# One pass over both expert tables for two of five blocks, in place of their row gathers

## The reference, cut to what matters

```python
q = (xs @ w_pq).reshape(PEER_BLOCK, PEER_HEADS, 2, PEER_QDIM // 2)
sc = jnp.einsum('thpd,hpnd->thpn', q, sub_keys)
s, i = lax.top_k(sc, PEER_TOPK)
cidx = i[:, :, 0, :, None] * PEER_KEYS + i[:, :, 1, None, :]
top, sel = lax.top_k(cand, PEER_TOPK)
eidx = jnp.take_along_axis(cidx, sel, axis=-1)
g = jax.nn.softmax(top, axis=-1)
hid = jnp.einsum('td,thkd->thk', xs, u_tab[eidx])
a = g * jax.nn.gelu(hid)
return jnp.einsum('thk,thkd->td', a, v_tab[eidx])
```

## Time and profile before

| what | value |
|---|---|
| median of 3 runs | 1980.1 us (1979.33 to 1987.95) |
| profiled execution, first to last instruction (span) | 1895.5 us |
| profiled execution, own time | not given apart; the span and what lies around it are compared with the median |
| PE busy, share of the span | 1601.3 us, 84% |
| DVE busy | 1263.2 us, 67% |
| ACT busy | 627.4 us, 33% |
| POOL busy | 1245.3 us, 66% |
| data moved | 744.60 MB, mean 393 GB/s |
| granted TensorE clock, mean | 0.964 |

### The profile page before, as it was taken

One profiled execution on the slowest core, in us unless ns is written; L12 is line 12 of the kernel. 1 busy time (PEld: TensorE's weight loads), 2 busy tenths in 40 slices (PEclk: granted clock), 3 DMA queues, 4 the chain that ended last, 5 costly groups with the idle time before them and its releaser, 6 DMA issues.

```text
span 1895.5 us, 20537 instructions
## 1 busy us (share of the span) xinstructions
PE 1601.3 (84%) x6192; PEld 881.4 (47%) x6192; DVE 1263.2 (67%) x2836; ACT 627.4 (33%) x1771; POOL 1245.3 (66%) x1199
## 2 busy tenths in 40 slices
PE   8999779879978698888898889998689877767877
PEld 7596445536435355355354465634436422222322
DVE  2379984576767755868587647589756897655543
ACT  1432561223237422232276222136522232222211
POOL 3027676576677755777777665677777777777771
PEclk9999999999989999999999998998899999999999
DMA  9899999999999999999999999999999999999995
GB/s 318 309 347 371 410 393 387 410 409 409 386 412 409 409 401 409 406 408 409 411 406 393 397 406 377 406 409 370 405 411 409 409 410 409 409 409 409 410 409 225
DMA packets 210197, 744.60 MB, mean 393 GB/s; under 512 B 24640, under 2 KB 29544, under 8 KB 209960
## 3 DMA queue, kind: packets, MB, share of 16 engines
q0 software_dynamic: 166720, 605.75, 80.9%
q1 hardware_dynamic: 43368, 137.53, 19.0%
HBM read 736.03 MB, written 7.75 MB: 392 GB/s over the span
## 4 chain that ended last, share of the span: by engine, by line
DMA 35%; PE 30%; POOL 20%; issue 9%; DVE 6%; ACT 1%; SPq 0%; DVEq 0%; ACTq 0%
DMA vbuf<-in_peer_v,idx 18%; PE acc L959 10%; POOL ubuf L1670 9%; POOL vbuf L1670 8%; DMA ubuf<-in_peer_u,idx 8%; PE mixer L667 5%; DMA held<-in_peer_u,idx 4%; PE mixer L833 2%; PE mixer L936 2%; DVE ubuf L1598 2%; PE mixer L683 2%; DMA wring<-in_c_k 1%; POOL wring L1670 1%; DMA held<-in_peer_v,idx 1%; POOL held L1670 1%
## 5 line engine op out<-in xcount | busy, mean ns | idle before, releaser
L959 PE MATMUL acc<-vbuf,diag 128*128 128x512 f32 x1308 | 644.5, 627 | 159.5 <-DMA vbuf<-in_peer_v,idx 154.6
L1670 POOL DMA_INDIRECT ubuf<-in_peer_u,idx x518 | 553.9, 1069 | 255.5 <-issue 138.4
L1670 POOL DMA_INDIRECT vbuf<-in_peer_v,idx x478 | 512.4, 1072 | 264.4 <-PE acc L959 133.0
L1598 DVE CUSTOM_DVE_ANT_0 ubuf<-ubuf,x 128x1024 f32<-128x1024 f32 x332 | 404.9, 1224 | 252.9 <-DMA ubuf<-in_peer_u,idx 249.7
L959 PEld LDWEIGHTS acc<-vbuf,diag 128*128 128x128 f32 x1308 | 236.7, 196 | 470.4 <-issue 429.0
L1598 DVE CUSTOM_DVE_ANT_0 ubuf<-ubuf,mixer 128x1024 f32<-128x1024 f32 x186 | 225.6, 1218 | 118.2 <-DMA ubuf<-in_peer_u,idx 81.9
L1200 ACT ACTIVATE act_h<-hid 128x4 f32<-128x4 f32 x144 | 29.5, 205 | 504.1 <-DVE hid L1598 503.4
L936 PEld LDWEIGHTS mixer<-stage,wring 128*128 128x128 f32 x1280 | 149.5, 193 | 17.4 <-issue 15.4
L936 PE MATMUL mixer<-stage,wring 128*128 128x128 f32 x1280 | 150.6, 276 | 0.7 <-DMA wring<-in_w_pq 0.6
L1229 ACT ACTIVATE diag<-ident,coef 128x128 f32<-128x128 f32 x392 | 138.4, 395 | 22.1 <-PE acc L959 18.1
L1610 DVE SCALAR_TENSOR_TENSOR y_acc<-vbuf,coef,y_acc 128x1024 f32<-128x1024 f32 x99 | 127.3, 1286 | 18.1 <-DMA vbuf<-in_peer_v,idx 16.0
(11 more groups left out here) (266 smaller groups left out, 1959.1 us busy)
## 6 DMA issues: line engine op xcount, KB each, us to landing
wring<-in_w_pq SPq DMA_DIRECT2D x80, 512.0 KB, 8.1
wring<-in_w_qk SPq DMA_DIRECT2D x66, 512.0 KB, 7.6
wring<-in_w_out SPq DMA_DIRECT2D x40, 512.0 KB, 7.5
wring<-in_w_v SPq DMA_DIRECT2D x20, 512.0 KB, 7.5
ubuf<-in_peer_u,idx POOLq DMA_INDIRECT x518, 13.0
vbuf<-in_peer_v,idx POOLq DMA_INDIRECT x478, 12.7
wring<-in_c_k SPq DMA_DIRECT2D x8, 512.0 KB, 6.9
wring<-in_c_v SPq DMA_DIRECT2D x8, 512.0 KB, 7.9
```

Of the source, the lines that this page charges most:

```text
L959: last = pe.matmul(sums[hf], diags[D_PLAN[n][0]], v_buf[b][:, hf * 512:(hf + 1) * 512], start=first, stop=last_one)
L1598: nc.vector.tensor_tensor_reduce(out=u, in0=u, in1=x, scale=1.0, scalar=0.0, op0=ALU.mult, op1=ALU.add, accum_out=hid[:, k % MARKS:k % MAR ...
L1670: pool.indirect_dma_start(buf, None, a[table], bass.IndirectOffsetOnAxis(ap=idx[p % 2][:, at:at + 1], axis=0)).then_inc(landed_, 16)
```

## The change

Blocks 2 and 3 are no longer gathered. Slots remain for blocks 0, 1 and SMP (`GATHERED`), so `JSLOTS` is 2 x 128 + 64 = 320. For blocks 2 and 3 (`DENSE`, 256 frames together) a new lane "d" reads both tables once, as 128 tiles of 128 experts each. All mixers move forward: each takes 51 slots, SMP 60, and the pass begins at mark `SWEEP = 219` and ends at mark 323. Before it, in marks 198 to 219, the first part of the gates is built.

The gates of the pass are a matrix over 256 frames and 16384 experts, held in `big` for 52 tiles at a time and filled in four chunks of tiles (0 to 43, 44 to 71, 72 to 99, 100 to 127). For each chunk there are 64 groups of 4 frames. DVE makes one-hot rows `hot_j` (128 x 512) and `hot_i` (128 x 4w, w being the width of the chunk) by comparing with `iota`; one of two groups is scaled by the gate on DVE, the other on ACT; PE multiplies them (4 products with w columns), and ACT copies the result into `big`. `hot_j` has two buffers and `hot_i` three. Chunks 1 to 3 run inside the pass, in 22 tiles each.

`held` shrinks to one tile (`HELD = 1`). The room comes from `kv`, `q_pad` and `sub_k`, which are now parts of `big`. The sample's search takes 4 rounds in place of 8, with its halves of heads on halves of the partitions. v rows of slots from 206 on all go to DVE. The constant rows of the second LayerNorm are made once.

The core of the diff (lane names and marks, the sweep on each engine):

```diff
-HELD = 4
+HELD = 1
+GATHERED = (0, 1, SMP)
+DENSE = (2, 3)
+LAST_Q = len(GATHERED) - 1
+JSLOTS = LAST_Q * SLOTS + DEC
+SWEEP = 219
+MERGE = (SLOTS, SWEEP - V_LAG - 2)
 def on_tensor(k):
+    q = part_of(k)
+    return q < LAST_Q and q * SLOTS + 3 <= k < MERGE[q]
-BLOCK_1 = (5, 26), (26, 54), (54, 65), (65, 81), (70, 122)
-BLOCKS = (-30, 6), (6, 46), (46, 60), (60, 78), (66, 121)
+STAGES = {
+    1: ((5, 17), (17, 35), (35, 45), (45, 56), (48, 90)),
+    2: ((56, 68), (68, 86), (86, 96), (96, 107), (99, 141)),
+    3: ((107, 119), (119, 137), (137, 147), (147, 158), (150, 192)),
+    SMP: ((158, 170), (170, 197), (197, 207), (207, 218), (216, 242)),
+}
+CHUNKS = ((0, 44), (44, 72), (72, 100), (100, P))
+TOK = 4
+DRING_T = 7
+M_LAG, V_LAG_D = 2, 4
+def sweep_users():
+    users = [("t", q, 0) for q in range(len(DENSE))] + [("", 0, 0)] * 4 + [("g", 0, k) for k in range(GROUPS_D)]
+    users += [("x", 0, hf) for hf in range(2)]
+    for n in range(P + V_LAG_D):
+        if n + 1 < P:
+            users += [("x", n + 1, hf) for hf in range(2)]
+        users.append(("h", n, 0))
+        for c, (lo, hi) in enumerate(CHUNKS[1:], 1):
+            first, last = hi - HOMES + M_LAG, lo - 1
+            if first <= n <= last:
+                a, b = ((n + d - first) * GROUPS_D // (last + 1 - first) for d in (0, 1))
+                users += [("g", c, k) for k in range(a, b)]
...
+            def gains(u):
+                g_, w = G_INDEX[u], CHUNKS[u[1]][1] - CHUNKS[u[1]][0]
+                pe.wait_ge(hot_done, g_ + 1)
+                if g_ % 2 == 0:
+                    pe.wait_ge(hot_scaled, g_ // 2 + 1)
+                bank = bank_free(u)
+                for t in range(TOK):
+                    last = pe.matmul(bank[:, t * w:(t + 1) * w], hot_j[g_ % 2][:, t * P:(t + 1) * P],
+                                     hot_i[g_ % 3][:, t * w:(t + 1) * w], start=True, stop=True)
+            def turn_u(u):
+                raw = landed_tile("u", u[1])
+                bank = bank_free(u)
+                for c in range(4):
+                    at = (4 * u[2] + c) * P
+                    last = pe.transpose(bank[:, c * P:(c + 1) * P], raw[:, at:at + P], ident[:, :])
+            def hidden(u):
+                w = uT[u[1] % 2]
+                pe.wait_ge(bank_out, BANK_AT["x", u[1], 1] + 1)
+                bank = bank_free(u)
+                for c in range(KT):
+                    last = pe.matmul(bank[:, 0:DBLK], w[:, c * P:(c + 1) * P], x1T[:, c, :], start=c == 0, stop=c == KT - 1)
+            def spread(n):
+                w = landed_tile("v", n)
+                pe.wait_ge(mult_done, n + 1)
+                for q in range(len(DENSE)):
+                    for hf in range(2):
+                        last = pe.matmul(acc_d[q][hf], acts[n % ARING][:, q * P:(q + 1) * P], w[:, hf * 512:(hf + 1) * 512],
+                                         start=False, stop=n == P - 1)
...
+            def hots(u):
+                if g_ >= 2:
+                    dve.wait_ge(bank_done, BANK_AT[G_USERS[g_ - 2]] + 1)
+                nc.vector.tensor_tensor(hot_j[g_ % 2].rearrange("p (t n) -> p t n", n=P),
+                                        jig[:, 1, t0:t0 + TOK].unsqueeze(2).broadcast_to([P, TOK, P]),
+                                        iota[:, :].unsqueeze(1).broadcast_to([P, TOK, P]), ALU.is_equal)
...
+                        elif u[0] == "x":
+                            last = nc.scalar.copy(uT[u[1] % 2][:, u[2] * 512:(u[2] + 1) * 512], bank)
...
+                        else:
+                            last = nc.scalar.activation(acts[u[1] % ARING], bank[:, 0:DBLK], ACT.Gelu)
```

More of the change, by code:

```diff
@@ L139, with ring_plan @@
     PE_COUNT.append(PE_COUNT[-1] + on_tensor(_k))
-def ring_plan(count, first, more):
-    order, had, last, plan, n = list(range(first)), {}, {}, [], first
-    more = dict(more)
+def ring_plan(count, size, fewer_from):
+    order, had, last, plan = list(range(size)), [0] * size, [None] * size, []
     for k in range(count):
-        if k in more:
-            order = list(range(n, n + more[k])) + order
-            n += more[k]
+        if k == fewer_from:
+            order.remove(size - 1)
         b = order.pop(0)
         order.append(b)
[L152 to L160, removed]
+        plan.append((b, last[b], had[b]))
+        last[b], had[b] = k, had[b] + 1
+    return plan, last[size - 1]
+U_PLAN, U_LAST = ring_plan(JSLOTS, URING, SWEEP - 4)
+V_PLAN, V_LAST = ring_plan(JSLOTS, VRING, SWEEP - 4 - V_AT)
+D_PLAN, _ = ring_plan(PE_COUNT[JSLOTS], DRING, JSLOTS)
 def nkeys(p):
@@ new lines, with bank_plan @@
+USERS = sweep_users()
+G_USERS = [u for u in USERS if u[0] == "g"]
+G_INDEX = {u: n for n, u in enumerate(G_USERS)}
+BANKED = [u for u in USERS if u[0] in ("t", "g", "r", "x") or u[0] == "h" and u[1] < P]
+BANK_AT = {u: n for n, u in enumerate(BANKED)}
+def bank_plan():
+    plan, last, n = [], [None] * 4, 0
+    few = BANK_AT["x", 0, 0]
+    for m in range(len(BANKED)):
+        bank = m % 2 if m < few else (m - few) % 4
+        plan.append((bank, last[bank]))
+        last[bank] = m
+    return plan
@@ new lines, with home_pieces @@
+BANK_PLAN = bank_plan()
+CHUNK_OF = [next(c for c, (lo, hi) in enumerate(CHUNKS) if lo <= n < hi) for n in range(P)]
+D_STEPS = len(USERS) + 3
+TILES = []
+for _n in range(-1, P + V_LAG_D):
+    if _n + 1 < P:
+        TILES.append(("u", _n + 1))
+    if _n >= V_LAG_D:
+        TILES.append(("v", _n - V_LAG_D))
+TILE_AT = {t: n for n, t in enumerate(TILES)}
+def home_pieces(c):
+    lo, hi = CHUNKS[c]
+    out = []
+    while lo < hi:
+        n = min(hi - lo, HOMES - lo % HOMES)
+        out.append((lo, lo % HOMES, n))
+        lo += n
+    return out
@@ L209, in spans, with sweep_marks @@
+def sweep_marks():
+    before = USERS.index(("x", 0, 0))
+    out = [198.0 + (k + 0.5) * (SWEEP - 198.0) / before for k in range(before)]
+    cost = [{"h": 3.5, "x": 0.6, "g": 0.6, "r": 0.6}[u[0]] for u in USERS[before:]] + [1.0] * 3
+    at, total = 0.0, sum(cost)
+    for c in cost:
+        out.append(SWEEP + (at + 0.5 * c) * (JSLOTS + 3.0 - SWEEP) / total)
+        at += c
+    return out
 def spans():
@@ L350, in build @@
         rowid = sb("rowid", [P, 2, SLOTS])
+        row_d = [sb(f"row_d{n}", [P, 2, SLOTS]) for n in range(len(DENSE))]
+        g_d = [sb(f"g_d{n}", [P, SLOTS]) for n in range(len(DENSE))]
         g_next = sb("g_next", [P, SLOTS])
@@ L362, in build @@
         mv2 = sb("mv2", [P, 2, 2])
+        statd = sb("statd", [P, 2, 2, 6])
+        mvd_all = sb("mvd", [P, 2, 2])
+        mvd = [mvd_all[:, n, :] for n in range(2)]
+        rstdd = sb("rstdd", [P, 2])
         rstd2 = sb("rstd2", [P, 2, 2])
@@ L565, in x_sync @@
                     sp.dma_start(lam_v[:, :, :].rearrange("p c n -> p (c n)"), a["lam"]).then_inc(s_lamin, 16)
[L566 to L569, removed]
-                    sp.dma_start(held[:, t, :], a["w_v"][t]).then_inc(held_in, 16)
+                if p == 0 and (kind, i) == ("qk", 4):
+                    for t in range(HELD):
+                        sp.dma_start(held[:, t, :], a["w_v"][t]).then_inc(held_in, 16)
         def sample_bias(sp, h):
@@ L908, in o_tensor @@
             for c in range(KT):
[L909 removed]
+                last = pe.transpose(ps_s[:, c * P:(c + 1) * P], x1[p][:, c * P:(c + 1) * P], ident[:, :])
             last.then_inc(x1T_done, 1)
@@ L1251, in c_scalar @@
-            yield
-            act.wait_ge(sc_out, HEADS * NB)
-            act.wait_ge(y_done, SMP - 1)
-            for hf in range(2):
-                nc.scalar.copy(ps_s[:, hf * 512:(hf + 1) * 512], x1[SMP % 3][:, hf * 512:(hf + 1) * 512]).then_inc(x_copied, 1)
-            yield
+            of = part_of(mid_slots(p).start)
+            act.wait_ge(x1_done, GATHERED[of] + 1)
+            act.wait_ge(v_out, 2 * (p + 1))
+            for hf in range(2):
+                last = nc.scalar.copy(x_mid[:, hf * 512:(hf + 1) * 512], x1[GATHERED[of]][:, hf * 512:(hf + 1) * 512])
@@ L1260, in x_vector, with e_scalar @@
+        def e_scalar(act, _):
+            for t in range(4):
+                if t == 1:
+                    for q in range(len(DENSE)):
+                        act.wait_ge(lnd_v, q + 1)
+                        nc.scalar.activation(rstd[:, q:q + 1], mvd[q][:, 1:2], ACT.Sqrt, bias=eps[:, 0:1]).then_inc(lnd_r, 1)
+                yield
         def x_vector(dve, p, chain):
```

527 lines of the change are left out of this document (360 added, 167 removed).

## The result

The changed kernel took 2543.2 us (median of 4, 2534.2 to 2551.2), the kernel before 1980.3 us beside it: 1.284 times as long (95% interval 1.279 to 1.289). I had forecast 2530 us, with PE as the bound.

A forecast was written before the change was run, and what follows sets the result against it. PE was taken to bound everything behind the first 150 us: 1189 us ahead of the pass, 1168 pass, 70 wait and 35 end make 2462 us; plus 84.6 gives 2547, shaded to 2530, range 2410 to 2680 us.

The forecast's parts named there:

- The bytes: Whole kernel: 268.4 MB removed, 134.2 and 6.3 MB added, 744.6 MB falling to 616.7 MB.
- The pass: Blocks 2 and 3: PE bounds it, 7.78 us a tile, 996 us, plus 172 us of gates, 1168 us.
- The one wait: Pass, third gate group of a tile: `hots` waits for a `hot_j` buffer, 70 us over 66 tiles, between 0 and 165.
- the clock falls in the pass: Rival, pass: waits draw the clock from 1.00 to 0.88, costing about 160 us, 2690 us in all; chance 0.05.
- Ahead of the pass: Stretch before the pass: 1085 us of PE work plus 104 us idle, so the pass runs freely after 1189 us.
- What I wrote of the mixers: Mixer stage of 51 slots ahead of the pass: PE needs 226 us, the transfers 191 us.
- The end: After the pass: residual, constant rows, last v rows, LayerNorms and a store, 35 us, between 20 and 45.
- What lies around the span: Whole execution: the 84.6 us between the old span and the median of runs is added to the new span.
- memory stayed no bound: Rival, whole kernel: PE keeps up with 4.6 us a tile and 616.7 MB set the time, 1654 us; chance 0.03.
- The handshake of the gates: Rival, pass: gate groups run one after the other, 170 us more than the sum, about 2700 us; chance 0.12.
- The mixers did compress: Rival, ahead of the pass: mixer chains keep half their slack, 40 us more a mixer, 2690 us; chance 0.12.
- The rule with fp32 spaced like bf16: Pass: 216 ns per 512-column matmul whatever the type gives some 2.8 us a tile, with memory the bound.

The follow-up runs named there:

- a_order: Changed kernel with PE doing the `spread` products after a tile's first gate group, not ahead of all its groups: 2410.2 us.
- c_halfv: Changed kernel loading only the left half of each v tile of the pass, 33.5 MB less: 2529.3 us.
- e_rows: Changed kernel with every third gathered v row that PE adds in blocks 0 and 1 given to DVE (66 of 200): 2501.9 us.
- g_bf16: a_order with bf16 operands in `hidden` and `spread`, ACT copying each v tile: 2043.1 us, 1.035 times the kernel before beside it.

## Why the prediction was right

**The bytes**: 616.7 MB forecast, 617.4 measured.

**The pass**: right in kind and in its largest term. 996 us for 128 tiles stand against 1006 with residual and constant rows, and 1168 for all records against 1171 in a_order. The spacing of 256 columns, which could not be read before and was put at 0.217 us on the line between its neighbours, is (3.62 - 0.38) / 15 = 0.216 us. That memory, DVE and ACT lie hidden under it is shown by c_halfv for memory, and by a_order's pass without idle time for the others.

**The one wait**: 70 us forecast, 45 us of idle measured in the pass. Beside it stood something that I had made a rival with a chance of 0.05 and a price of 160 us: the clock falls in the pass. It fell, for part of the time, and cost 73 us. My step failed in taking one full-clock stretch without gaps for a pass in which every second tile has a gap and three groups of narrow records in a row. Narrow records as such were in that stretch too, 32 of 64 columns in turn with 8 of 512, and its clock was 1.00. The timeline of the kernel before there:

```profile
1181.10 3.68 PE L667 MATMUL mixer<-xT,wring 128*128 128x64 f32 x32
1184.61 3.65 PE L959 MATMUL acc<-vbuf,diag 128*128 128x512 f32 x8
1188.10 3.68 PE L667 MATMUL mixer<-xT,wring 128*128 128x64 f32 x32
```

Wait and clock together are 118 us, where the sum had 70.

**Ahead of the pass**: 1189 us forecast, 1224 measured. PE was busy 1136 us and not 1085, idle 88 and not 104. By line the excess of 51 us is this: the v rows took 398.5 us and not 358, so the 1.79 us a row was a term too small (1.99 measured, close to the 1.98 of the kernel before); chunk 0 took 81 and not 57; all the rest took 657 and not 670. The clock of 0.94 has a part in it, but no run varied the clock alone there. On the other chips the pass began at 1203 to 1210 us, 14 to 21 over the forecast. What I wrote of the mixers, that PE bounds them, holds only in part. e_rows took 114 us of PE work away and began the pass 21 to 26 us earlier.

**The end**: 36 us against 35.

**What lies around the span**: the step that was plainly wrong. I took the difference of 84.6 us between the median of the runs and the span of the profiled execution for a cost around every execution. No run shows such a cost; what lies around a span is 2 us. The 84.6 us fit what the same kernel differs by between chips (1898 us in one comparison, 1967 to 1986 in three). The sum inside the span, 2462 us, was 87 us short of 2549.3: 35 ahead of the pass, 51 in it and 1 at the end. The two errors cancelled by luck, and the 2530 us are closer than their working deserved.

**The rivals**: memory stayed no bound (c_halfv). The handshake of the gates alone bounded nothing: a_order has the same buffers and waits, and no idle time in its pass. The mixers did compress: idle time ahead of the pass was 88 us, under the 104 of the sum. The rule with fp32 spaced like bf16 fails by the rows: `spread` in fp32 has two records of 0.43 us for a product of 512 columns, and in g_bf16 one, 4 of them in 1.03 us, (1.03 - 0.38) / 3 = 0.217 each. The Trainium skill (TensorE: Matmul & The Clock Gate, Back-to-back issue gap) has 216 ns for an isolated matmul of 512 columns, and the bf16 row agrees with it, the fp32 row does not. The same section has some 131 ns for a sustained stream of them, which neither row bears out. With bf16 in every product of the pass but the transposes, the pass is bound by memory and the kernel is faster, so that rival named the right condition.

## What to carry to other kernels

Before bytes are traded for arithmetic, sum the records on the engine that gets the arithmetic, by spacing and with the records per product of the type; here 127 MB saved, worth some 320 us at 393 GB/s, cost 1171 us of fp32 products while only 264 v rows, some 450 us back to back, were taken off PE. Try whether narrow products can stand among wide ones: moving one call was worth 118 us of this pass, 4.6% of the kernel. And compare an execution's span with the median only when both come from the same chip.

## What the runs showed of the hardware

- The granted clock fell though PE was busy for 843 of 888 us. Over the changed kernel's tiles 22 to 99, most with three groups of 28 columns in a row and a gap of 0.39 or 1.10 us, it was 0.93 on average; with the `spread` products between the first group and the others, at the same records and without a gap, 1.00. In g_bf16, where the groups are about half of a tile, it was 0.77 with PE idle for 12% of the pass; in the version with bf16 groups and moved rows, 0.89 with PE idle for 30%. So the idle share alone doesn't put these in order. What does was not varied alone.
- When work was taken off PE its clock was lower: 0.78 and not 0.87 in the last stretch ahead of the pass. With the waits that came in, some four fifths of the freed time were lost.
- An fp32 record of 28 columns is spaced like one of 128: 16 in 1.86 us, (1.86 - 0.27) / 15 = 0.106 us. In bf16, 4 records of 28 columns took 0.25 us, (0.25 - 0.17) / 3 = 0.027 each. A group of 28 columns costs 8 x 0.106 us in fp32 and 4 x 0.027 in bf16, and the number of columns changes little of it in fp32.
- The same kernel took 1980, 1898, 1967 and 1986 us in the four comparisons, while it waited for memory. The changed one took 2543 and 2540 us in two of them, the first and the third.
